# Second mixer of a hybrid trunk: triangular solve without W, half-width levels, transposed powers by transposes

## The reference, cut to what matters

```python
kk = jnp.einsum('...id,...jd->...ij', kc, kc)
M = jnp.eye(C) + jnp.where(strict, bc[..., :, None] * kk * decay, 0.0)
W = triangular_solve(M, (bc * gam)[..., None] * kc, ...)
U = triangular_solve(M, bc[..., None] * vc, ...)
qk = jnp.einsum('...id,...jd->...ij', qc, kc) * decay

def step(S, xs):
    u_ = U_ - einsum('bhck,bhkv->bhcv', W_, S)
    o_ = einsum('bhck,bhkv->bhcv', qd_, S) + einsum('bhij,bhjv->bhiv', qk_, u_)
    S = gl_[..., None, None] * S + einsum('bhck,bhcv->bhkv', kd_, u_)
```

## Time and profile before

| | us |
|---|---|
| median of 3 runs (1418.02 to 1422.92) | 1419.03 |
| the profiled execution's own time | 1421.18 |
| its span | 1419.4 |
| PE busy (share of the span) | 1378.4 (97%) |
| PEld busy | 1167.3 (82%) |
| DVE busy | 690.3 (49%) |
| ACT busy | 498.2 (35%) |
| POOL busy | 373.6 (26%) |
| f32 products of `chunks` (L2008), x1152 records | 146.5 |
| `turn` (L2014), x224 records | 33.5 |
| fill parts (L1999), 3 x 448 records | 87.1 + 86.7 + 86.6 |

### The profile page before, as it was taken

One profiled execution on the slowest core, in us unless ns is written; L12 is line 12 of the kernel. 1 busy time (PEld: TensorE's weight loads), 2 busy tenths in 40 slices (PEclk: granted clock), 3 DMA queues, 4 the chain that ended last, 5 costly groups with the idle time before them and its releaser, 6 DMA issues.

```text
span 1419.4 us, 28320 instructions
## 1 busy us (share of the span) xinstructions
PE 1378.4 (97%) x11820; PEld 1167.3 (82%) x11820; DVE 690.3 (49%) x981; ACT 498.2 (35%) x711; POOL 373.6 (26%) x464
## 2 busy tenths in 40 slices
PE   9999899999999999999999999998899999999997
PEld 7776588888888888878888888887788888888886
DVE  5356643333333323677787787786443333333222
ACT  5233444223223322334345344435242322323221
POOL 1003412122122001453354344445021221221010
PEclk9999999999999999999999999999999999999999
DMA  6657522432223231200120120210232223223311
GB/s 229 214 170 249 157 90 90 153 112 90 90 108 132 86 119 59 90 31 31 60 90 31 60 90 31 90 60 16 104 112 97 89 89 118 89 100 122 122 42 61
DMA packets 32046, 140.92 MB, mean 99 GB/s; under 512 B 4538, under 2 KB 6842, under 8 KB 20059
## 3 DMA queue, kind: packets, MB, share of 16 engines
q1 hardware_dynamic: 31962, 139.75, 28.5%
HBM read 128.63 MB, written 11.11 MB: 98 GB/s over the span
## 4 chain that ended last, share of the span: by engine, by line
PE 87%; DVE 8%; issue 1%; DMA 1%; ACT 1%; POOL 1%; SPq 1%; DVEq 0%; POOLq 0%; ACTq 0%
PE P L1619 59%; PE P L1999 9%; PE P L2008 8%; DVE arena L1366 2%; PE P L2014 2%; PE P L2213 1%; DVE wl L1399 1%; PE P L2191 1%; PE P L2180 1%; PE P L2151 1%; PE P L1848 1%; PE P L1716 1%; DMA arena<-bias_scratch 1%; DVE arena L1348 1%; DVE arena L1415 0%
## 5 line engine op out<-in xcount | busy, mean ns | idle before, releaser
L1619 PE MATMUL P<-zh,wh 128*128 128x260 f16 x1712 | 329.9, 274 | 1.3 <-DVE wl L1105 1.2
L1619 PE MATMUL P<-zl,wh 128*128 128x260 f16 x1712 | 329.8, 274 | 0.0
L1619 PE MATMUL P<-zh,wl 128*128 128x260 f16 x1712 | 329.6, 274 | 0.0
L1085 DVE SCALAR_TENSOR_TENSOR wl<-stage,wh 128x2048 f16<-128x2048 f32 (+1 forms) x76 | 187.3, 2465 | 199.9 <-ACT wh L705 196.0
L1619 PE MATMUL P<-arena,wh 128*128 128x260 f16 x1832 | 278.5, 273 | 1.6 <-DVE arena L1348 0.8
L1619 PEld LDWEIGHTS P<-arena,wh 128*128 128x128 f16 x1832 | 177.1, 97 | 29.7 <-issue 2.4
L1619 PEld LDWEIGHTS P<-zh,wh 128*128 128x128 f16 x1712 | 164.6, 97 | 33.3 <-issue 5.5
L1619 PEld LDWEIGHTS P<-zh,wl 128*128 128x128 f16 x1712 | 165.9, 97 | 26.2
L1619 PEld LDWEIGHTS P<-zl,wh 128*128 128x128 f16 x1712 | 165.7, 97 | 26.1
L1619 PE MATMUL P<-arena,wl 128*128 128x260 f16 x916 | 176.0, 273 | 0.0
L705 ACT ACTIVATE wh<-stage 128x2048 f16<-128x2048 f32 (+1 forms) x82 | 165.6, 2020 | 6.6 <-PE P L1619 3.6
(11 more groups left out here) (342 smaller groups left out, 1631.7 us busy)
## 6 DMA issues: line engine op xcount, KB each, us to landing
stage<-w_gu SPq DMA_DIRECT2D x44, 1024.0 KB, 4.8
stage<-w_in SPq DMA_DIRECT2D x23, 1024.0 KB, 4.9
stage<-w_dn SPq DMA_DIRECT2D x16, 1408.0 KB, 5.9
arena<-cache_k SPq DMA_DIRECT2D x32, 256.0 KB, 3.4
stage<-w_out SPq DMA_DIRECT2D x8, 1024.0 KB, 5.8
arena<-cache_v SPq DMA_DIRECT2D x32, 256.0 KB, 3.0
arena<-delta_state SPq DMA_DIRECT2D x8, 512.0 KB, 3.7
o_ds<-arena SPq DMA_DIRECT2D x8, 512.0 KB, 6.9
```

The costliest lines, as they stand in the source:

```text
L1085: nc.vector.scalar_tensor_tensor(out=wl[:, j, 0:words], in0=stage[:, j, 0:words], scalar=WS, in1=wh[:, j, 0:words], op0=MUL, op1=SUB).then ...
L1619: mm = nc.tensor.matmul(pm[j][:, c, :], w[:, wslot, o:o + 128], x[:, k, c * CH:(c + 1) * CH], start=(k == first and w is wh and x is xh), ...
```

## The change

For each head and chunk, W is not computed. R = beta V - kbg^T S is formed in place of bV (DVE), T R is a product of its own (bank 6), and ScalarE copies it to the operand of the state and output products. With W go the transpose of kbg, its copy `Kp`, the product and its copy. The transposed powers of D are made by transposes of the copied powers (`turn`) instead of products. The levels compute and subtract only the half of the columns that changes (`late`, `packed`), in place in `yb`. The outer product goes from level 2 to behind the first T R product, into banks 4 and 5. Fill parts, convolutions, `leave`, `stat_head`, the ScalarE split and silu, and the DVE split quarters change places. In the diff the indentation is cut by eight, and unchanged lines are mostly left out.

```diff
--- before.py
+++ after.py
@@ -35,7 +35,7 @@
-OUT1_CALLS = (2, 3, 4, 5, 8, 10, 12)
+OUT1_CALLS = (2, 3, 4, 5, 6, 8, 10)
@@ -59,12 +59,12 @@
 HEAD_TILES = {
-    "pe": ["gb_ps", "kk_ps", "qk_ps", "n_ps", "tk_ps", "tkb_ps", "d2_ps", "dt2_ps", "d4_ps", "dt4_ps", "y2_ps",
-   "d8_ps", "y3_ps", "tv_ps", "y4_ps"] + ["x_ps", "z_ps", "v_ps"] * 3 + ["u_ps", "w_ps", "ds_ps"] +
-  ["ws_ps", "ds_ps"] * 3 + ["o_ps"],
-    "act": ["gam", "gd", "et", "kd4", "nf", "kd", "d2", "d4", "dt4", "d8", "bv", "x", "x", "x", "w", "o"],
-    "dve": ["ex", "bd", "kb", "nt", "dt", "d", "at", "y1", "dt2", "kp", "y2", "y3", "xt"] + ["z", "xt"] * 3 +
-   ["u", "s"] * 4,
+    "pe": ["gb_ps", "kk_ps", "qk_ps", "n_ps", "tk_ps", "d2_ps", "dt2_ps", "y2_ps", "d4_ps", "dt4_ps", "y3_ps", "tv_ps",
+   "d8_ps", "y4_ps"] + ["x_ps", "z_ps", "v_ps"] * 3 + ["u_ps", "ds_ps"] + ["ws_ps", "u_ps", "ds_ps"] * 3 +
+  ["o_ps"],
+    "act": ["gam", "gd", "et", "kd4", "nf", "kd", "d2", "d4", "dt4", "d8", "bv", "x", "x", "x"] + ["u"] * 4 + ["o"],
+    "dve": ["ex", "bd", "kb", "nt", "dt", "d", "at", "y1", "dt2", "y2", "y3", "xt"] + ["z", "xt"] * 3 +
+   ["s"] + ["r", "s"] * 3,
@@ -306,6 +306,14 @@
     return bass.AP(tensor=apad[g].tensor, offset=apad[g].offset, ap=[apad[g].ap[0], [36, NDEC], [1, H0]])
+def late(l, ap):
+    return ap.rearrange("p (b two s) -> p b two s", two=2, s=16 << l)[:, :, 1, :]
+def packed(l, ap):
+    return ap.rearrange("p (b s) -> p b s", s=16 << l)
@@ -1001,12 +1009,11 @@
         silu_z(h)
+        silu_v(h)
...
         evac(ddt, 7, "dt4_ps", "dt4", h)
-        silu_v(h)
         evac(d2_8, 6, "d8_ps", "d8", h)
@@ -1023,17 +1030,21 @@
                 nc.scalar.activation(krow[0:36, :], P[0:36, 4, 264:392], ACT.Copy).then_inc(krow_s, 1)
+                if p < HG:
+                    next_split("in1", p, 0)
...
         if p < HG:
-            next_split("in1", p, 0)
-        evac(kbg_w, 4, "w_ps", "w", h)
-        if p < HG:
             silu_qk(p)
-        act.preload_act_table_set("natural_log_exp_and_others")
-        if p < HG:
-            norm_l2(p)
+        for c in range(4):
+            act.wait_ge(*G("u_ps", 4 * h + c + 1))
+            nc.scalar.activation(nf_u[:, c * 128:(c + 1) * 128], P[:, 6, c * 128:(c + 1) * 128], ACT.Copy
+                                 ).then_inc(S["u"], 1)
+            if c == 0:
+                act.preload_act_table_set("natural_log_exp_and_others")
+            if c == 2 and p < HG:
+                norm_l2(p)
@@ -1407,12 +1418,9 @@
-    def add(dst, bank, src, ready, name, count, op=ADD):
+    def add(dst, bank, src, ready, name, count):
         dve.wait_ge(*G(ready, count))
-        if op == ADD:
-            nc.vector.tensor_tensor(dst, P[:, bank, :], src, ADD).then_inc(S[name], 1)
-        else:
-            nc.vector.tensor_tensor(dst, src, P[:, bank, :], SUB).then_inc(S[name], 1)
+        nc.vector.tensor_tensor(dst, P[:, bank, :], src, ADD).then_inc(S[name], 1)
@@ -1450,7 +1458,7 @@
         v = dS[:, h % 2, :].rearrange("p (c n) -> p c n", c=2)
-        nc.vector.tensor_tensor(v, P[:, 2:4, :], v, ADD).then_inc(snew, 1)
+        nc.vector.tensor_tensor(v, P[:, 4:6, :], v, ADD).then_inc(snew, 1)
@@ -1481,6 +1489,8 @@
         nc.vector.tensor_tensor(kbg_w, P[:, 3, :], k, MUL).then_inc(S["kb"], 1)
+        convolve(h, 2, 0)
+        convolve(h, 2, 1)
@@ -1500,16 +1510,12 @@
             head_scale(n)
+        convolve(h, 2, 2)
+        convolve(h, 2, 3)
...
         nc.vector.tensor_copy(dt2_x, P[:, 6, :]).then_inc(S["dt2"], 1)
-        dve.wait_ge(*G("tkb_ps", h + 1))
-        nc.vector.tensor_copy(Kp, P[:, 4, :]).then_inc(S["kp"], 1)
-        for i in range(2):
-            convolve(h, 2, i)
...
         add(yb, 2, ya, "y2_ps", "y2", h + 1)
-        for i in range(2, 4):
-            convolve(h, 2, i)
@@ -1523,50 +1529,52 @@
         for l in range(3):
-            src, dst = (yb, ya) if l % 2 == 0 else (ya, yb)
             dve.wait_ge(*G("z_ps", 3 * h + l + 1))
-            nc.vector.tensor_copy(nt_z, P[:, 7, :]).then_inc(S["z"], 1)
+            nc.vector.tensor_copy(nt_z[:, 0:256], P[:, 7, 0:256]).then_inc(S["z"], 1)
...
                     convolve(p, 0, 3)
-                elif l == 2:
-                    leave(p, 2)
...
             dve.wait_ge(*G("xt", 4 * h + l + 1))
-            add(dst, 6, src, "v_ps", "xt", 3 * h + l + 1, SUB)
+            dve.wait_ge(*G("v_ps", 3 * h + l + 1))
+            nc.vector.tensor_tensor(late(l, yb), late(l, yb), packed(l, P[:, 6, 0:256]), SUB
+                                    ).then_inc(S["xt"], 1)
...
             elif l == 1:
-                decode_rows(h)
...
                     convolve(p, 1, 2)
-            else:
-                decode_state(h)
-                if h == 0:
-                    gate_pieces()
-        dve.wait_ge(*G("u_ps", h + 1))
-        nc.vector.tensor_copy(nf_u, P[:, 5, :]).then_inc(S["u"], 1)
+                decode_rows(h)
+        if p < HG:
+            leave(p, 2)
+        decode_state(h)
+        if h == 0:
+            gate_pieces()
...
                 dve.wait_ge(*G("ws_ps", 3 * h + c))
-                dve.wait_ge(*G("u", 4 * h + c))
-                nc.vector.tensor_tensor(nf_u[:, cc], nf_u[:, cc], P[:, 2, cc], SUB).then_inc(S["u"], 1)
+                nc.vector.tensor_tensor(bV[:, cc], bV[:, cc], P[:, 2, cc], SUB).then_inc(S["r"], 1)
+                if p < HG and c == 1:
+                    split_quarter(FIRST_UNIT["in1"] + 2 * p + 2, 0, 1)
+                    split_quarter(FIRST_UNIT["in1"] + 2 * p + 2, 0, 2)
+                if p < HG and c == 2:
+                    split_quarter(FIRST_UNIT["in1"] + 2 * p + 2, 0, 3)
...
                 nc.vector.tensor_copy(dst, P[:, 3, cc]).then_inc(S["s"], 1)
+                if p < HG:
+                    split_quarter(FIRST_UNIT["in1"] + 2 * p + 2, 0, 0)
...
                                                op0=MUL, op1=ADD).then_inc(S["s"], 1)
-            if p < HG:
-                split_quarter(FIRST_UNIT["in1"] + 2 * p + 2, 0, c)
+        if p < HG - 1:
+            leave(p, 3)
...
             add_query(h)
-        if p < HG - 1:
-            leave(p, 3)
@@ -2020,8 +2028,6 @@
         pe.wait_ge(nqq, HG)
-        ready(HG - 1, "w")
-        pe.wait_ge(*G("u", 4 * (HG - 1) + 1))
@@ -2088,11 +2094,9 @@
         mm.then_inc(S["gb_ps"], 1)
-        if 1 <= h < HG - 1:
+        fill(3)
+        if h >= 1:
             pe.wait_ge(nln, h + 1)
-            stat_head(h - 1)
-        fill(3)
-        if h == HG - 1:
@@ -2108,23 +2112,25 @@
         turn(5, k, "tk_ps")
-        ready(h, "kbg")
-        turn(4, kbg_w, "tkb_ps")
...
         chunks(2, ddt, dd, "d2_ps")
-        chunks(6, dd, ddt, "dt2_ps")
         fill(3)
-        ready(h, "d2", "dt2", "nf", "at")
-        chunks(3, dt2_x, d2_8, "d4_ps")
-        chunks(7, d2_8, dt2_x, "dt4_ps")
+        ready(h, "d2")
+        turn(6, d2_8, "dt2_ps")
...
         chunks(2, d2_8, ya, "y2_ps")
+        ready(h, "dt2", "nf")
+        chunks(3, dt2_x, d2_8, "d4_ps")
         fill(3)
-        ready(h, "d4", "dt4", "y2", "kp", "kd")
-        chunks(6, ddt, dd, "d8_ps")
+        ready(h, "d4", "at")
+        turn(7, dd, "dt4_ps")
+        ready(h, "y2")
         chunks(4, dd, yb, "y3_ps")
+        ready(h, "kd")
...
         turn(5, v, "tv_ps")
+        ready(h, "dt4")
+        chunks(6, ddt, dd, "d8_ps")
@@ -2139,22 +2145,22 @@
         for l in range(3):
-            src = yb if l % 2 == 0 else ya
             pe.wait_ge(*G("xt", 4 * h + l + 1))
-            turn(5, src, "x_ps")
+            turn(5, yb, "x_ps")
             pe.wait_ge(*G("om", 3 * h + l + 1))
-            chunks(7, offs[l], src, "z_ps")
-            fill(2)
-            if l == 2:
-                pe.wait_ge(um_s, h + 1)
-                for c in range(2):
-                    mm = nc.tensor.matmul(P[:, 2 + c, :], krow[32 * c:32 * c + 4, :],
-                                          um[32 * c:32 * c + 4, :], start=True, stop=True)
-                mm.then_inc(outer_ps, 1)
+            for c in range(4):
+                cc = slice(c * 128, (c + 1) * 128)
+                mm = nc.tensor.matmul(packed(l, P[:, 7, c * 64:(c + 1) * 64]), offs[l][:, cc],
+                                      late(l, yb[:, cc]), start=True, stop=True)
+            mm.then_inc(S["z_ps"], 1)
+            fill(1 if l == 2 else 2)
...
             pe.wait_ge(*G("z", 3 * h + l + 1))
-            chunks(6, dt2_x, nt_z, "v_ps")
-            fill(2 if l == 2 else 1)
+            for c in range(4):
+                mm = nc.tensor.matmul(P[:, 6, c * 64:(c + 1) * 64], dt2_x[:, c * 128:(c + 1) * 128],
+                                      nt_z[:, c * 64:(c + 1) * 64], start=True, stop=True)
+            mm.then_inc(S["v_ps"], 1)
+            fill(1)
@@ -2165,39 +2171,48 @@
         pe.wait_ge(*G("xt", 4 * h + 4))
+        def pseudo_values(c):
+            cc = slice(c * 128, (c + 1) * 128)
+            nc.tensor.matmul(P[:, 6, cc], yb[:, cc], bV[:, cc], start=True, stop=True).then_inc(S["u_ps"], 1)
```

(34 more changed lines are left out.)

## The result

The changed kernel takes 1412.88 us (median of 7, 1407.15 to 1414.18) against 1420.75 for the kernel before on the same chips (median of 7, 1418.02 to 1423.02): ratio 0.993, 95% interval 0.9911 to 0.9949. It is 8 us faster; 21 were forecast.

The account below looks back on a forecast made before the run. PE, busy 97% of the span, was taken to bound heads 0 to 6, the dependent chain head 7. Seven heads at 2.6 us (18.2) plus 3.4 make 21.6; median 1419.03 becomes 1397.4, rounded to 1398, range 1385 to 1410.

Parts of the forecast that it names:

- Direction and work on PE: Per head, 2.24 us of PE instructions leave for certain, plus 0.5 from half columns; chance of faster 0.89.
- the sum: Stage times added per head, 48.6 us against 51.2, and over all heads 21.6 us saved.
- The column term: In the levels, 48 records at 64 columns take 0.101 us each instead of 0.1115, saving 0.5 us per head.
- The port wait before D4: DVE's V convolutions, held by POOL's mask products, delay dt2's copy; PE waits 1.5 us, ends 0 and 2.3.
- The first stage: Head start to first x transpose: PE savings of 1.35 us are spent on waiting, 24.53 becomes 24.6.
- The levels: First x transpose to pseudo-value product: 16.17 us becomes 12.05, z copy in time, 0.2 of waits, 1.7 real gain.
- the walk: Step-by-step timing of the new instruction order through head 3 and head 7; it gives the first stage 24.6 us.
- The chunk loop of heads 0 to 6: Loop grows from 10.51 to 11.95 us; longer chain hidden but for 0.15 per chunk.
- rival D: Chunk loop: split quarters set the chain, PE waits 4.5 us more per head, total slower at 1429; chance 0.05.
- Head 7: Last head, set by its dependent chain: earlier levels, chunks of 2.7 us, loop's end 3.4 us earlier.
- Rival C: Unseen small waits, 0.2 per level and chunk, eat half the gain: 1.2 us per head, 1406; chance 0.16.
- the doubled case: Small unseen waits in levels and chunks at twice 8.4 us less gain, giving 1415.

Follow-up runs that it names:

- the first experiment: Changed kernel with convolution 2 of Q of the next head moved behind the z copy of level 0: 1407.85 us, ratio 0.9892.
- the repaired kernel: Changed kernel with Q's convolution 2 behind the z copy, V's convolutions 2 and 3 behind Y2's addition, V silu between D4 and dt4 copies: 1399.79 us.

## Why the prediction was wrong

- **Direction and work on PE: right.** Removed work was 2.24 + 0.31 us a head, where the sum had 2.24 + 0.5.
- **The column term: right in kind, 0.2 too high.** 0.105 us a record where I took 0.101 and a price by columns had 0.056. I had each level's chain 0.5 shorter but gave this no price of its own; full width would have shown as 1.2 us of waits, so the term was mostly a latency term.
- **The port wait before D4: right in kind, time and place**, 1.5 forecast, 1.67 measured. The first stage came out at 24.86 against 24.6. Removing it gave 0.96, not 1.5, since the V silu came next.
- **The levels: the step that failed.** "gate_lo now covers the slow convolution instead of the long POOL state product, and the copy comes in time" was decided by two events 0.02 us apart, 25 us into the head, and the walk, whose times are good to 0.3, put no time to them. In heads 1 to 6 the convolution comes 0.02 us behind the state product, in head 0 0.22, and head 7 has none. So the 0.64 us wait of before, which the sum took as gone, stayed (0.65 by the first experiment), and records (0.19) and small waits (0.18 above the 0.2 allowed) added the rest of the 1.0 us by which the levels missed. In heads 1 to 6 that makes 6 of the 9 missing us; most of the rest are 0.26 in the first stage and 0.18 in the chunk loop of each head. That a convolution 0.02 us earlier would have escaped the hold is not shown; that behind the copy it costs PE nothing is (first experiment).
- **The chunk loop of heads 0 to 6: right**, 12.13 against 11.95. The longer chain is hidden, with 0.16 us of wait a chunk, and rival D, the split quarters in the chain, didn't come.
- **Head 7: wrong by 3.6.** 0.8 ahead of the levels: D8's copy ends 0.3 later than in the walk, and Y3's addition ends 0.4 after it, behind a weight split that POOL held for 4.69 us instead of 2.49; the walk had no hold there. 0.9 from levels of 3.76 us each instead of 3.45. The remaining 1.9 lie in the loop, and I put them down to the clock, for which the sum had no term: at full clock the last chunk took the 2.6 forecast, the two that half clock touched about 3.75 each. Why the clock fell is open.
- **1.6 us more ahead of the second mixer**, where the kernels are the same. In the first 190 us the trace of before has about 13.6 us at half clock and the one after about 17.2; that this is the cause is likely, but no experiment shows it.

Rival C, half the gain eaten by small waits, was the nearest in time: 1406 and, doubled, 1415. I gave it 0.16 and ended the range at 1410, short of the doubled case. Its mechanism came only in part: one wait of 0.64 us made the largest part of each head's miss, with small ones beside it. That the repaired kernel measures 1399.79, close to the forecast 1398, is luck: its heads take 47.77 us against the forecast 48.6, because the foreseen wait at D4 is gone too, and head 7 and layer 0 take that back.

## What to carry over

When PE is the bound, price an edit as instructions removed minus waits changed, and check each wait of the old trace for whether it really goes: here 2.55 us of work bought 1.17. Where DVE and POOL both read SBUF, an order that depends on a few hundredths of a microsecond is to be taken at its worse side, or made independent of it by putting the PSUM copy that PE waits for ahead of the SBUF work. A stage without filler is priced by its chain, and at both levels of the clock: the clock of a stage in the old trace (1.00 here) need not be the one in the new (0.50 for 6.8 us).

## What was not expected of the hardware

- The granted clock fell to 0.50 in head 7's loop in the changed kernel and cost about 1.1 us in each of two chunks. With 4.0 us of extra products in the loop it fell for 3.4 us, which is also what the repaired kernel has without them; with three parts moved out of the levels, for 13.7 us.
- Single-chunk copies from PSUM on ScalarE take 0.28 us (L1042), not the 0.37 of the scaled form in the earlier trace rows.
